# P·V and the spatial gate: one plain float32 product in place of three products of high and low parts

## What is computed

```python
def _forgetting_attention(q, k, v, log_f):          # 6 heads of 64
    ...
    p = jax.nn.softmax(s, axis=-1).astype(v.dtype)
    return jnp.einsum('bhqk,bkhd->bqhd', p, v)

def _diff_attention(q, k, v, lam, lam_init, norm_g): # 4 heads of 64, two maps each
    ...
    p = jax.nn.softmax(s, axis=-1)
    a = (p[:, :, 0] - lam * p[:, :, 1]).astype(v.dtype)
    return jnp.einsum('bhqk,bkhe->bqhe', a, v)

def _chunked_spatial_gating(z, ln_g, ln_b, w_s, b_s): # 6 heads, chunks of 128
    ...
    w = jnp.tril(w_s)
    mixed = jnp.einsum('hts,bcshd->bcthd', w, g) + jnp.transpose(b_s)[None, None, :, :, None]
    return u * mixed.reshape(b, s, SGU_WIDTH)
```

## Time and profile before

| | |
|---|---|
| three runs | 1958.74 us median (1956.76 to 1958.92) |
| profiled execution | 1957.5 us, its span 1955.8 us, granted clock 0.991 |
| PE busy | 1886.8 us (96%) |
| DVE busy | 1471.7 us (75%) |
| ACT, POOL busy | 713.8 us (36%), 337.5 us (17%) |
| chain that ended last | PE 85%, DVE 7%, ACT 2%, DMA 1% |

### The profile page before, as it was taken

One profiled execution on the slowest core, in us unless ns is written; L12 is line 12 of the kernel. 1 busy time (PEld: TensorE's weight loads), 2 busy tenths in 40 slices (PEclk: granted clock), 3 DMA queues, 4 the chain that ended last, 5 costly groups with the idle time before them and its releaser, 6 DMA issues.

```text
span 1955.8 us, 25136 instructions
## 1 busy us (share of the span) xinstructions
PE 1886.8 (96%) x9125; PEld 1579.8 (81%) x9125; DVE 1471.7 (75%) x2185; ACT 713.8 (36%) x1074; POOL 337.5 (17%) x291
## 2 busy tenths in 40 slices
PE   6999999999989999999999999999998999999996
PEld 6888888888778888888888888888887788888884
DVE  6777777954776787777887777886567777777778
ACT  4242333435544324233234233334355442423331
POOL 6200000153314500000160000003333252000002
PEclk9999999999989999999999999999998999999998
DMA  5222223236732223222322222232566232222231
GB/s 219 84 110 86 107 86 129 106 112 189 197 87 74 93 106 115 86 107 86 130 86 108 86 107 86 107 136 82 169 186 171 55 108 85 109 86 107 86 129 43
DMA packets 41929, 217.09 MB, mean 111 GB/s; under 512 B 8724, under 2 KB 9172, under 8 KB 17928
## 3 DMA queue, kind: packets, MB, share of 16 engines
q1 hardware_dynamic: 38984, 200.35, 28.9%
q0 software_dynamic: 2880, 15.90, 3.5%
HBM read 198.28 MB, written 17.93 MB: 111 GB/s over the span
## 4 chain that ended last, share of the span: by engine, by line
PE 85%; DVE 7%; issue 2%; ACT 2%; DMA 1%; SPq 1%; POOL 1%; DVEq 0%; ACTq 0%; POOLq 0%
PE psum L969 78%; PE psum L1166 3%; DMA rawA<-in_a_w 1%; DVE res L1433 1%; PE psum L1262 1%; PE psum L997 1%; SPq L443 1%; DVE hl L1810 1%; DVE st L1457 1%; DVE negm L1783 1%; PE psum L1250 1%; PE psum L1264 1%; ACT psum L893 0%; DVE hl L1510 0%; PE psum L1238 0%
## 5 line engine op out<-in xcount | busy, mean ns | idle before, releaser
L969 PE MATMUL psum<-xhi,whiA 128*128 128x512 f32 (+1 forms) x768 | 288.0, 375 | 10.3 <-DVE xlo L1412 10.3
L969 PE MATMUL psum<-whiD,hl 128*128 128x512 f32 x832 | 283.8, 390 | 3.5 <-DVE hl L1510 2.8
L969 PE MATMUL psum<-xlo,whiA 128*128 128x512 f32 (+1 forms) x768 | 286.3, 373 | 0.0
L969 PE MATMUL psum<-xhi,wloA 128*128 128x512 f32 (+1 forms) x768 | 286.3, 373 | 0.0
L969 PE MATMUL psum<-xhi,whiB 128*128 128x512 f32 x704 | 273.9, 389 | 0.0
L969 PE MATMUL psum<-xlo,whiB 128*128 128x512 f32 x704 | 273.9, 389 | 0.0
L969 PE MATMUL psum<-xhi,wloB 128*128 128x512 f32 x704 | 273.9, 389 | 0.0
L774 ACT ACTIVATE s<-psum 128x512 f32<-128x512 f32 x36 | 21.5, 598 | 576.2 <-PE psum L969 576.2
L1531 DVE SCALAR_TENSOR_TENSOR nat<-psum,nat 128x1024 f32<-128x1024 f32 x144 | 175.7, 1220 | 26.5 <-PE psum L969 26.5
L1531 DVE SCALAR_TENSOR_TENSOR res<-psum,res 128x1024 f32<-128x1024 f32 x108 | 132.0, 1222 | 76.1 <-PE psum L969 76.1
L969 PEld LDWEIGHTS psum<-whiD,hl 128*128 128x128 f32 x832 | 156.2, 188 | 39.5 <-DVE hl L1510 4.5
(11 more groups left out here) (212 smaller groups left out, 3643.4 us busy)
## 6 DMA issues: line engine op xcount, KB each, us to landing
rawA<-in_a_w SPq DMA_DIRECT2D x63, 1024.0 KB, 6.3
rawB<-in_b_w SPq DMA_DIRECT2D x54, 1024.0 KB, 4.7
rawD<-in_d_w SPq DMA_DIRECT2D x46, 1024.0 KB, 4.7
stacks<-hl SPq DMA_DIRECT2D x192, 64.0 KB, 1.7
whiD<-stacks POOLq DMA_DIRECT2D x10, 768.0 KB, 6.1
wloD<-stacks POOLq DMA_DIRECT2D x10, 768.0 KB, 5.7
gbr<-in_gb_row SPq DMA_DIRECT2D x7, 1024.0 KB, 8.6
stacks<-wloD SPq DMA_DIRECT2D x48, 64.0 KB, 1.7
```

The lines of the kernel that those rows point to most:

```text
L969: ins = t_.matmul(out_, a_, b_, start=(start and k == 1), stop=(stop and k == n), skip_group_check=check)
```

## The change

P·V takes one plain float32 matmul of 64 columns for each key block; the gate's product takes one plain float32 matmul of 256 columns for each head. What made the low parts for them goes: `p_lo`, the first half of `output`, `values(j)` on DVE (low parts of V), `ghi`, `glo`, `wshi`, `wslo`. `p_hi` becomes `p_out`, the same copy into a float32 tile. `vals` halves in size; `thi` and `tlo`, which shared its place in the SwiGLU stages, get places of their own, and a wait of DVE on `rows_put` goes with that. Semaphores follow: the banks of `natural` are given back by ACT's copy, and PE waits for `f_ok` ahead of the second projection.

```diff
-        hl = sb("hl", [P, 9, 512], F32R)
-        vals = sb("vals", [P, NT, 2, FOX_W + DIFF_W], F32R)
+        hl = sb("hl", [P, 10, 512], F32R)
+        vals = sb("vals", [P, NT, FOX_W + DIFF_W])
+        thi = sb("thi", [P, 3 * 512], F32R)
...
-        pthi = [hl[:, 4, :], hl[:, 5, :]]
-        ptlo = [hl[:, 6, :], hl[:, 7, :]]
+        pt = [s32[:, 1, :], s32[:, 3, :]]
...
-                        a.activation(vhi[:, t, at:at + n_], src[:, lo:lo + n_], ACT.Copy).then_inc(vhi_ok, 1)
+                        a.activation(vals[:, t, at:at + n_], src[:, lo:lo + n_], ACT.Copy).then_inc(nat_free["AAB"[j]], 1)
...
-                        act.wait_ge(ws_tri, l + 1)
-                        a.activation(wshi, wsr, ACT.Copy).then_inc(wshi_ok, 1)
...
-                        act.wait_ge(gb_ok, NT * l + NT)
-                        a.activation(ghi, nat[:, :, 0:SGU_W], ACT.Copy).then_inc(ghi_ok, 1)
...
-                    a.activation(pthi[G % 2][:, 0:w], bank[4 + G % 2][:, 0:w], ACT.Copy).then_inc(pthi_ok, 1)
+                    a.activation(pt[G % 2][:, 0:w], bank[4 + G % 2][:, 0:w], ACT.Copy).then_inc(p_ok, 1)
...
-                    pe.wait_ge(pt_ok, l * ALL + G + 1)
+                    pe.wait_ge(p_ok, l * ALL + G + 1)
                     vc = PAIRS[b] * 2 * HD + hh * HD
-
-                    both = bank[4 + G % 2][:, 0:2 * HD].rearrange("p (a n) -> p a n", a=2)
                     for e in range(t + 1):
-                        t_.matmul(both, pthi[G % 2][:, e * P:e * P + P], vals[:, e, :, vc:vc + HD],
-                                  start=(e == 0), stop=(e == t), skip_group_check=True)
-                        ins = t_.matmul(both[:, 0, :], ptlo[G % 2][:, e * P:e * P + P], vhi[:, e, vc:vc + HD],
-                                        start=False, stop=(e == t), skip_group_check=True)
+                        ins = t_.matmul(bank[4 + G % 2][:, 0:HD], pt[G % 2][:, e * P:e * P + P], vals[:, e, vc:vc + HD],
+                                        start=(e == 0), stop=(e == t))
...
-                pe.wait_ge(wslo_ok, l + 1)
-                pe.wait_ge(glo_ok, l + 1)
+                pe.wait_ge(ws_tri, l + 1)
+                pe.wait_ge(gb_ok, l * NT + NT)
...
-                    ins = product(o, [((wshi[:, h * P:h * P + P], wslo[:, h * P:h * P + P]),
-                                       (ghi[:, :, h * HD:h * HD + HD], glo[:, :, h * HD:h * HD + HD]))])
+                    ins = t_.matmul(o, wsr[:, h * P:h * P + P], nat[:, :, h * HD:h * HD + HD], start=True, stop=True)
...
-                def p_lo(G):
-                    w_ = (G % NT + 1) * P
-                    dve.wait_ge(pthi_ok, l * ALL + G + 1)
-                    v.tensor_tensor(ptlo[G % 2][:, 0:w_], bank[4 + G % 2][:, 0:w_], f32(pthi[G % 2][:, 0:w_]),
-                                    ALU.subtract).then_inc(pt_ok, 1)
...
-                    v.tensor_scalar(olo[:, G % 2, :], b_[:, HD:2 * HD], rinv[:, j, 0:1], None, ALU.mult).then_inc(olo_ok, 1)
-                    dve.wait_ge(olo_ok, l * ALL + G + 1)
-                    v.scalar_tensor_tensor(out=o, in0=b_[:, 0:HD], scalar=rinv[:, j, 0:1], in1=olo[:, G % 2, :],
-                                           op0=ALU.mult, op1=ALU.add).then_inc(o_ok, 1)
+                    v.tensor_scalar(o, b_[:, 0:HD], rinv[:, j, 0:1], None, ALU.mult).then_inc(o_ok, 1)
```

More of the change, by code:

```diff
@@ L293, in build @@
         pt_done = sem("pt_done")
-        pthi_ok = sem("pthi_ok")
-        pt_ok = sem("pt_ok")
+        p_ok = sem("p_ok")
         pv_done = sem("pv_done")
-        olo_ok = sem("olo_ok")
         o_ok = sem("o_ok")
@@ L316, in build @@
         hlf = hl[:, :, :].rearrange("p a n -> p (a n)")
[L317 to L320, removed]
         x32 = [s32[:, c // 2, (c % 2) * HALF:(c % 2) * HALF + HALF] for c in range(NC)]
-        vhi, vlo = vals[:, :, 0, :], vals[:, :, 1, :]
         mixr = mix[:, 0:MIX]
@@ L329, in build @@
         sums = s32[:, 0:2, :].rearrange("p a (b n) -> p (a b) n", b=2)
-        valf = vals[:, :, :, :].rearrange("p t a n -> p (t a n)")
-        thi, tlo = valf[:, 0:3 * 512], valf[:, 3 * 512:6 * 512]
+        tlo = hlf[:, 7 * 512:10 * 512]
         tsum = mix[:, 0:3 * 512]
@@ L511, in _ @@
             done(g.memset(mone[:, :], -1.0))
-            done(g.memset(vals[0:1, 0:2, 0, 0:S].bitcast(F32), -1.0))
+            done(g.memset(vals[0:1, 0:2, 0:S], -1.0))
             done(g.memset(mv[:, :, :], 0.0))
@@ L783, in seven @@
                     act.wait_ge(t_ok, 4 * n + 4)
-                    a.activation(thi, tsum, ACT.Copy).then_inc(thi_ok, 1)
+                    a.activation(thi[:, :], tsum, ACT.Copy).then_inc(thi_ok, 1)
                     act.wait_ge(used["B"], l * BU_ALL + f * BU_FFN2 + i + 1)
@@ L894, in exp, with p_out @@
                                      accum_out=rsum[:, i:i + 1]).then_inc(exp_ok[m], 1)
-                def p_hi(G):
+                def p_out(G):
                     w = (G % NT + 1) * P
@@ L929, in _ @@
                     if G:
-                        p_hi(G - 1)
+                        p_out(G - 1)
                     if k == 0 and b + 1 < BODIES:
@@ L945, in _ @@
                             wo_half("D", l * D_ALL + D_WO, k - NT)
-                p_hi(ALL - 1)
+                p_out(ALL - 1)
                 act.wait_ge(wo_b_done, l + 1)
@@ L1332, in natural @@
                     pe.wait_ge(nat_free["A"], l * 2 * NT + min(j, 1) * NT + AHEAD)
+                    if j == 1:
+                        pe.wait_ge(f_ok, l * NT + NT)
                     if halved:
@@ L1585, in seven @@
                     dve.wait_ge(thi_ok, n + 1)
-                    v.tensor_tensor(tlo, tsum, f32(thi), ALU.subtract).then_inc(tlo_ok, 1)
+                    v.tensor_tensor(tlo, tsum, f32(thi[:, :]), ALU.subtract).then_inc(tlo_ok, 1)
                     for h in range(2):
@@ L1679, in key @@
                     v.tensor_tensor(stage(b)[3], bank[7][:, :], f32(stage(b)[2]), ALU.subtract).then_inc(qk_ok, 1)
[L1681 to L1692, removed]
+                for t in range(NT):
+                    dve.wait_ge(nat_free["A"], l * 2 * NT + t + 1 + AHEAD)
+                    v.tensor_tensor(flog[:, t, :], bank[t + NAT_BANK[0]][:, F_AT:F_AT + FOX_H], f_bias, ALU.add).then_inc(f_ok, 1)
                 dve.wait_ge(f_ok, l * NT + NT)
@@ L1703, in _ @@
                     v.bn_aggr(gmv[:, t, :], gst[:, t, :]).then_inc(gmv_ok, 1)
-                dve.wait_ge(wshi_ok, l + 1)
-                v.tensor_tensor(wslo, wsr, f32(wshi), ALU.subtract).then_inc(wslo_ok, 1)
                 split("A", l * A_ALL + A_NATS[1])
@@ L1720, in _ @@
                     v.tensor_tensor(nat[:, t, 0:SGU_W], nat[:, t, 0:SGU_W], sgu_b, ALU.add).then_inc(gb_ok, 1)
-                dve.wait_ge(ghi_ok, l + 1)
-                v.tensor_tensor(glo, nat[:, :, 0:SGU_W], f32(ghi), ALU.subtract).then_inc(glo_ok, 1)
                 dve.wait_ge(chi_ok, l + 1)
@@ L1727, in _ @@
                 split("A", l * A_ALL + A_NATS[2])
-                values(1)
-                values(2)
                 for h in range(SGU_H):
@@ L1840, in _ @@
                         mix(G)
-                    if G:
-                        p_lo(G - 1)
                     if k == 0 and b + 1 < BODIES:
@@ L1856, in _ @@
                 early_add(6)
-                p_lo(ALL - 1)
                 early_add(7)
```

10 lines of the change are left out of this document (1 added, 9 removed).

## The result

| | us, median (lowest to highest) |
|---|---|
| before, four runs on the same chip | 1958.83 (1956.76 to 1959.01) |
| changed, four runs | 1940.39 (1938.95 to 1941.27) |
| ratio | 0.9911, 95% interval 0.9897 to 0.9925 |

A forecast was written before the change was run, and what follows sets the result against it. PE, busy 96%, was taken as the bound, with DVE pacing the diff bodies. Terms -15.1 + 3.0 - 4.0 + 0 + 1.3 - 0.9 = -15.7 us gave 1941.8 profiled, 1943.0 us as median; range 1924 to 1956.

The forecast's parts named there:

- Step 1: Heads: without `p_lo` on DVE, `values` is released sooner and the next `row_max` comes forward; -15.1 us over two layers.
- Bodies: Signs by head body: body 1 from 27 to about 25 us, 3 from 33 to about 29, others under 1 each.
- Step 2: Weight fills in bodies 1 and 2: ACT waits for `rawA`, so part of the gain is given back; +3.0 us.
- Step 3: `output` loses one DVE instruction, mostly covered in diff steps; -4.0 us, mostly for body 3, ends 0 and -10.
- Step 4: PE's price of P·V: a key block stays at 0.22 us with plain float32 loads; 0 us.
- Dear loads (slower): Rival at `values`: plain float32 weight loads cost more, 0.44 us a block; +20 us, 1979 us; chance 0.10.
- the 142 ns of the low end: P·V loads as short as the transposes' plain float32 loads, 142 ns against 197, making 0.11 us a block.
- Step 5: Gate's product as 12 records at 0.215 us: +1.3 us; `project(1)`'s wait for low parts of V goes: -0.9 us.
- Step 6: Removed `ghi`, `wshi`, `glo`, `wslo`, low parts of V, PE's wait for `f_ok`, moved `thi` and `tlo`: nothing.
- a wait for a wait: Rival at `values`: ACT's copy, behind one or two exps, comes as late as `p_lo` did; about 1955 us; chance 0.10.
- More than that: Rival: PE wins back all the weight loader's 30.0 us ahead of `values`, fills following; about 1928 us; chance 0.22.

The follow-up runs named there:

- DVE's time put back: Changed kernel with an unread row maximum over ACT's copy of P at `p_lo`'s place on DVE, `values` not waiting for it: 1949.17 us, 0.9971.
- the late release: Changed kernel with `values` waiting for a one-element DVE memset at `p_lo`'s place instead of ACT's copy: 1943.22 us, 0.9930.
- taking the wait down to 1.4 us: Changed kernel with ACT's conversion of the next query weights (`query_half`) one step later in bodies 0 to 2: 1937.19 us, 0.9903.
- P·V alone: Changed kernel with the gate back in three products of parts, so only P·V is plain float32: 1937.50 us, 0.9896.
- unread subtraction: Changed kernel with a subtraction of `p_lo`'s size put back at its place on DVE, result unused, `values` not waiting for it: 1957.12 us, 1.0000.

## Why the prediction held, step by step

- **Step 1, `p_lo` off the path, -15.1 us: right.** Without `p_lo` alone the kernel before gains 14.3 us. The prediction also said why: the next `row_max` comes forward. The runs bear this out: DVE's time put back costs up to 12.2 us, the late release about 4. Where the gain falls was only half right (Bodies, below).
- **Step 2, +3.0 us given back at the weight fills: failed.** ACT does wait for `rawA` longer and in body 1 too (0.60 us at 505.60), as was said. But body 2 fell by 1.6 us in layer 0 (0.9 in layer 1), where only about 0.9 were granted; without `p_lo` alone 14.3 us came, where 15.1 less 3.0 would have left 12.1; and taking the wait down to 1.4 us changed nothing. The step took the 50.6% of SP and the fill in body 2's chain for a bound; it was one of two paths of like length. Where the fill did cost is a place the step left out, body 0 of layer 0, which grew by 0.9 us behind one long put of SP.
- **Step 3, -4.0 us for `output`: not settled.** Alone, in the kernel before, it gives 1.3 us, less than its own interval: there DVE waits for exp behind it, as the row of step 11 showed. With `p_lo` gone the rest of P·V's change gives 5.8 us, and `output` is one part of that; its share is not shown.
- **Step 4, PE's price of P·V, 0: right.** Blocks stand 0.22 us apart, and the plain loads are as long as the `F32R` ones. Dear loads (slower) fall with this, the 142 ns of the low end too. By the four passes that the Trainium skill gives for true float32 (FP8 and Floating Point Precision, TensorE Precision Notes) alone, an estimated 5 us would have been added over 200 blocks. Nothing of it is seen: the loads are 0.11 us apart, where a record of 64 columns was put at 0.054.
- **Step 5, the gate, +1.3 and -0.9: right** in the price of a record, 0.215 us, and in the wait that went; the sum of the two, 0.4, is below what a run tells (0.9995 alone).
- **Step 6, nothing: not contradicted**; not tried one by one.
- **Bodies.** 1 as said, 3 in layer 0 only. A longer body 0 was named as a sign of dear loads; in layer 0 it came, with blocks at 0.22 us, so the loads are not its cause. Body 4 was to change by under 1 us and fell by 2.2 in each layer. The prediction read from 28.95 of 30.0 us busy that PE had no slack there. Busy time counts matmuls to modelled ends that overlap, so a full row is not a full pipeline, and DVE, whose busy time in that window fell by 7.2 us (21.50 to 14.30), was not looked at. The body's chain before has more of DVE than of PE. With `p_lo` alone removed body 4 takes 19.1 us, as in the changed kernel.

The miss of 2.7 us is about the size of step 2: without its +3.0 the sum is -18.7, and 18.4 and, run again, 18.7 were measured. That the total comes so close is partly luck, for 4.4 us of it came from body 4, where the prediction allowed under 2, and body 3 of layer 1 gave 2 us less than it said. The parts timed alone, 14.3 for `p_lo`, 1.3 for `output` and 0.5 for the gate, make 16.1 us; P·V alone gives 20.1 on the chip where `p_lo` gave 14.3. The 4.5 us by which P·V exceeds `p_lo` and `output` timed alone is at the limit of what the three intervals allow; whether `output` is worth more with `p_lo` gone, or another piece of P·V counts, is open. Of the rivals, a wait for a wait is seen as 4.3 us in nine waits, against 14.8 for `p_lo`. More than that did not come: 30.0 us of the loader's waiting were never all on the path.

## What to carry to other kernels

Splitting a number into high and low parts costs more than the matmuls: the work that makes the low part stands in another engine's queue, and where that queue sets the pace of a loop its time is the price, even if nobody waits for its result. With weights of 128 by 128 and 64 columns the loads, 0.11 us apart, set PE's price here, so one plain float32 product took the place of two `F32R` matmuls at the same 0.22 us. And a chain's share of a line is not what its removal brings: 24.4% of a chain was worth nothing here, because the path beside it was as long.

## What was not expected of the hardware

The unread subtraction has both operands in SBUF, where `p_lo` had one in PSUM. Alone it takes what its width asks, 0.28 us for 128 columns. Beside a subtraction on POOL it does not. DVE and then POOL in the timeline of that kernel:

```profile
483.85 1.96 DVE L1769 TENSOR_TENSOR hl<-s 128x128 fp32r<-128x128 f32 x1 [1.67 <-ACT s L880]
```

```profile
483.28 2.38 POOL L606 TENSOR_TENSOR wloA<-rawA,whiA 128x1024 fp32r<-128x1024 f32 x1 [3.98 <-ACT whiA L694]
```

POOL ends at 485.66 and DVE 0.15 us later, at 485.81. The same is seen at 471.83 (1.72 us), 520.00 (1.58) and 531.98 (1.95), each ending 0.14 or 0.15 us after POOL's instruction, while subtractions of the same width that meet no work of POOL take 0.28. The maximum with its one operand keeps 0.29 us beside the same instruction of POOL (at 470.93, where POOL works from 470.10 to 472.50). Nor is it the width that is written: `p_lo` itself, with one operand in SBUF and a result as wide, took 0.29 us in the kernel before at 484.41, where POOL works from 483.84 to 486.22. This is why the unread subtraction put in 17 us more than `p_lo` had taken. The Trainium skill says so (SBUF — State Buffer, Who interferes with whom): a DVE instruction with two SBUF inputs contends with a GpSimd instruction that reads SBUF, and one with at most one SBUF input, outside the two-port modes, does not. These rows agree.
